# Retention's norm in the first two layers: mean and gate in one VectorE pass, the inverse deviation applied by ScalarE

## The reference

```python
def retention_branch(q, k, v, gate, ret_decay, positions):
    q = rotary(q.reshape(B, S, RET_HEADS, RET_QK_DIM), positions, RET_THETA, RET_QK_DIM)
    k = rotary(k.reshape(B, S, RET_HEADS, RET_QK_DIM), positions, RET_THETA, RET_QK_DIM)
    ...
    o = fwd + bwd                                  # (1, 4 heads, 256 tokens, 512)
    mu = jnp.mean(o, axis=-1, keepdims=True)
    var = jnp.mean(jnp.square(o - mu), axis=-1, keepdims=True)
    o = (o - mu) * lax.rsqrt(var + EPS)
    o = jnp.transpose(o, (0, 2, 1, 3)).reshape(B, S, RET_HEADS * RET_V_DIM).astype(gate.dtype)
    return o * jax.nn.silu(gate)
```

## Time and profile before

| | us |
|---|---|
| median of 3 runs | 3060.93 |
| lowest and highest run | 3060.62, 3064.89 |
| the profiled execution | 3062.25 |
| its span in the trace | 3060.4 |

### The profile page before, as it was taken

The page is one execution under the profiler, slowest core; times in us unless marked ns, Lnnn a source line. Parts: engine busy times, 40 slices in busy tenths (PEclk is TensorE's granted clock), DMA queues, the critical chain, the costliest instruction groups (busy, mean ns, idle before and its releaser), DMA issues. The chain is left out here.

```text
span 3060.4 us, 49236 instructions
## 1 busy us (share of the span) xinstructions
PE 2916.6 (95%) x19366; PEld 2670.4 (87%) x19366; DVE 2271.7 (74%) x4037; ACT 1471.7 (48%) x2425; POOL 742.4 (24%) x374
## 2 busy tenths in 40 slices
PE   7899998999999898999998999999899999999998
PEld 7798887878898787999998988887799999988887
DVE  5878996687899766796568677777599557756665
ACT  3454333445433344545655455554454665445554
POOL 0100000010000000697776000001189776400000
PEclk9999998999999999999999999999899999999999
DMA  6445554543555452454443777873245443455554
GB/s 219 151 152 187 206 207 152 196 167 130 188 204 207 152 203 93 164 183 158 140 136 132 267 255 261 287 285 128 102 163 186 145 138 128 169 180 193 194 195 161
DMA packets 125976, 547.96 MB, mean 179 GB/s; under 512 B 13715, under 2 KB 17972, under 8 KB 101300
## 3 DMA queue, kind: packets, MB, share of 16 engines
q1 hardware_dynamic: 124572, 542.73, 50.8%
q10 hardware_dynamic: 1176, 2.10, 0.4%
HBM read 538.48 MB, written 6.29 MB: 178 GB/s over the span
## 5 line engine op out<-in xcount | busy, mean ns | idle before, releaser
L2011 POOL TENSOR_TENSOR q_lo<-q_raw,q_hi 128x1024 fp32r<-128x1024 f32 x250 | 678.6, 2725 | 226.3 <-ACT q_hi L2120 226.1
L2030 PE MATMUL k_psN<-k_hhi,q_hi 128*128 128x256 f32 x2304 | 665.6, 289 | 19.0 <-POOL q_lo L2011 18.1
L2030 PE MATMUL k_psN<-k_hhi,q_lo 128*128 128x256 f32 x2304 | 651.5, 283 | 0.0
L2030 PE MATMUL k_psN<-k_hlo,q_hi 128*128 128x256 f32 x2304 | 651.4, 283 | 0.0
L2120 ACT ACTIVATE q_hi<-q_raw 128x1024 fp32r<-128x1024 f32 x538 | 566.4, 1053 | 6.8 <-DMA q_raw<-up 4.1
L2030 PEld LDWEIGHTS k_psN<-k_hhi,q_hi 128*128 128x128 f32 x2304 | 441.1, 191 | 25.9 <-POOL q_lo L2011 21.9
L2323 DVE TENSOR_TENSOR q_lo<-q_raw,q_hi 128x1024 fp32r<-128x1024 f32 x288 | 352.8, 1225 | 132.0 <-ACT q_hi L2120 131.4
L2030 PEld LDWEIGHTS k_psN<-k_hlo,q_hi 128*128 128x128 f32 x2304 | 441.6, 192 | 0.0
L2030 PEld LDWEIGHTS k_psN<-k_hhi,q_lo 128*128 128x128 f32 x2304 | 441.1, 191 | 0.0
L744 DVE TENSOR_TENSOR k_wlo<-k_raw,k_whi 128x2048 fp32r<-128x2048 f32 x158 | 360.6, 2286 | 101.6 <-ACT k_whi L569 100.7
L569 ACT ACTIVATE k_whi<-k_raw 128x2048 fp32r<-128x2048 f32 x158 | 301.5, 1913 | 233.2 <-PE f_psA L421 102.9
(11 more groups left out here) (355 smaller groups left out, 5479.2 us busy)
## 6 DMA issues: line engine op xcount, KB each, us to landing
k_raw<-ws SPq DMA_DIRECT2D x180, 1024.0 KB, 4.8
q_raw<-down SPq DMA_DIRECT2D x288, 512.0 KB, 3.4
q_raw<-up SPq DMA_DIRECT2D x256, 512.0 KB, 4.2
k_x<-ada SPq DMA_DIRECT2D x48, 512.0 KB, 3.6
e_ada<-ada SPq DMA_DIRECT2D x48, 512.0 KB, 5.1
out<-k_x SPq DMA_DIRECT2D x3, 1024.0 KB, 3.9
k_x<-out SPq DMA_DIRECT2D x3, 1024.0 KB, 7.0
k_x<-x SPq DMA_DIRECT2D x2, 1024.0 KB, 6.0
```

The source lines that it names most:

```text
L2011: nc.gpsimd.tensor_tensor(lo[:, i % RING, :], raw[:, i % RING, :], hi[:, i % RING, :].bitcast(F32), ALU.subtract).then_inc(S["lo_pool"], 1)
L2030: last = nc.tensor.matmul(psD(n), w, h, start=kt == 0 and i == 0, stop=kt == KT - 1 and i == 2)
```

## The change

VectorE no longer waits for the inverse deviation. It writes (o - mean) x gate in one scalar_tensor_tensor for each half, straight behind the statistics (and the decay arguments, where there are any). ScalarE then multiplies `rog` in place by the inverse deviation, a value for each token, as the scale of a Copy. The count `r_og`, for which `ret_out` waits, is now raised by ScalarE, and VectorE's pass raises `acc_read`.

```diff
                         decay(1)
-                    elif name == "ret_values" and j < 2:
-                        decay(j + 2)
+                    elif name == "ret_values":
+                        if j < 2:
+                            decay(j + 2)
+                        act.wait_ge(S["r_rstd"], j + 1)
+                        for t in range(NT):
+                            act.wait_ge(S["acc_read"], n + t + 1)
+                            nc.scalar.activation(rog[:, t, :], rog[:, t, :], ACT.Copy, scale=RRS[:, 2 * j + t:2 * j + t + 1]).then_inc(S["r_og"], 1)
...
                         if j < 2:
                             decay_arg(j + 2)
-                        dve.wait_ge(S["r_rstd"], j + 1)
+                        own.wait()
+                        dve.wait_ge(S["r_var"], j + 1)
                         for t in range(NT):
-                            V.tensor_scalar(rog[:, t, :], o[t], MV[:, 4 * j + 2 * t:4 * j + 2 * t + 1], RRS[:, 2 * j + t:2 * j + t + 1],
-                                            ALU.subtract, ALU.mult).then_inc(S["acc_read"], 1)
-                        dve.wait_ge(S["acc_read"], n + 2)
-                        for t in range(NT):
-                            V.tensor_tensor(rog[:, t, :], rog[:, t, :], rg[:, j % 2, t, :], ALU.mult).then_inc(S["r_og"], 1)
+                            V.scalar_tensor_tensor(rog[:, t, :], o[t], MV[:, 4 * j + 2 * t:4 * j + 2 * t + 1], rg[:, j % 2, t, :],
+                                                   ALU.subtract, ALU.mult).then_inc(S["acc_read"], 1)
```

## The result

The changed kernel takes **3073.01 us** (median of 8 runs, 3068.76 to 3088.99) where the kernel before took 3062.79 in the runs beside it (median of 8): ratio 1.0033, 95% interval 1.0020 to 1.0046. A second set, 10 runs, gave 3072.27 and 1.0024 (1.0015 to 1.0034) against 33 runs of before. So the change costs 7 to 10 us. The forecast was 3064.1 with a range up to 3069: the sign was right, the size was not, and the time lies outside the range.

A forecast was written before the change was run, and what follows sets the result against it. VectorE, late from the first head on, was taken to set TensorE's restart at `conv_mean`. Lags of 2 x 0.59 + 2 x 0.20 = 1.58 us a layer, 3.2 in two, on 3060.93 gave 3064.1 us, range 3060 to 3069.

The forecast's parts named there:

- the sum: Both first layers: 2 x 1.58 = 3.2 us slower, bounds 2.2 to 4.6, giving 3064.1 us.
- What bounds the kernel: First layers: VectorE runs late from the first head on, and its last tap sets TensorE's restart at `conv_mean`, without slack.
- VectorE's new pass: Each head's norm: one pass per half of 0.75 us, the two ending 1.46 us after the statistics or decay arguments.
- ScalarE in front of L569: Each head: new ScalarE passes delay L569, so L744 is later by 0.59 us (heads 0, 1) and 0.20 (heads 2, 3).
- TensorE's wait before `cgate`: Before `cgate` in the first layer: TensorE's wait for L856 grows from 0.6 to near 2 us, costing nothing in itself.
- POOL: Inverse deviation in heads 2 and 3: POOL's pair still takes 0.19 and 0.69 us beside VectorE's new pass.
- TensorE's clock: Two stalls in each first layer: where the low clock falls is worth up to 0.85 us each, +/-3.4 us, no sign.
- The base: The whole kernel before the change: median of the runs 3060.93 us, to which the forecast effect was added.
- The saving gets through: Rival, chance 0.04: VectorE's 8.9 us a layer removes TensorE's stalls, 7.7 a layer, 15.4 in all, 3045.5 us.
- A longer low clock: Rival, chance 0.12: longer `cgate` wait may bring a low stretch, both restarts may fall badly; 6.6 us slower, 3067.5.
- Nothing moves: Rival, chance 0.03: ScalarE's passes overlap better than counted, or a later wait swallows the lag; 3061 us.
- POOL held up: Rival, chance 0.09: the new passes hold POOL off in each head, 6.6 us a layer, 13.2 slower in all, 3074.1.

The follow-up runs named there:

- half-width passes: The changed kernel with ScalarE's two new passes per head over the left 256 of 512 columns only; 3066.37 us in a single run.
- the taps moved as well: Changed kernel with ScalarE converting the next weights first and convolution taps thinned behind the fourth head, none in the last two units; 3055.27 us (share 0.5), 3054.07 us (0.75).

## Why the prediction was wrong

Three steps failed. The 19 runs of the changed kernel have a median of 3072.3, the forecast was 3064.1. Of the 8.2 us between them, 3.4 are the base, 0.8 are the price of ScalarE's pass, and 2.25 are low clock in the second block, a term that the sum put at nothing. The other 1.8 us are not explained.

**What bounds the kernel: right.** VectorE's last tap before `conv_mean` sets TensorE's restart; the lag added up over the four heads without loss (0.63 + 0.53 + 0.40 + 0.41 = 1.97).

**VectorE's new pass: right.** A pair of 1.40 to 1.41 us where 1.42 was forecast.

**ScalarE in front of L569: right in kind, short in size.** Taken from the end of L990 in head 0 (300.29), L749 starts at +3.93; the forecast said +3.95, and heads 0 and 1 were to lose 0.59 each and lost 0.57. From the end of L1013 in head 2 (378.61), POOL is ready at +1.06 and the first new pass starts at +1.09, as forecast, but L569 starts at +2.34 instead of +2.15 and L749 at +4.27 instead of +4.07. **The term that was mis-sized** is the new pass's price on ScalarE, taken from the Exp: "lasts 0.63 and lets the next start after 0.53". A pass takes 0.72 us, the pair 1.34, not 1.16, and L569 starts 1.25 behind its start, not 1.06. Heads 2 and 3 lose 0.40 each, twice the 0.20 of the sum. The new pass reads a value for each token beside its tile, the Exp does not, and the trace of the kernel before shows ScalarE operations of one size with and without such a value, L665 and L636:

```profile
L665 ACT ACTIVATE f_tmp<-f_tmp,f_stat 128x256 f32<-128x256 f32 x32 | 15.9, 500 | 3.1 <-DVE f_stat L959 3.1
...
L636 ACT ACTIVATE f_rt<-f_rt 128x256 f32<-128x256 f32 x1 | 0.4, 419 | 6.5 <-DVE f_rt L927 6.5
```

The two differ in more than this value, so it is only an estimate: 0.08 us more for each pass would have given 0.61 in place of 0.53; the spacing measured is 0.63 and 0.61. In heads 0 and 1 the error was hidden: the first pass could start at +0.75 in place of +0.83. The stage's lag, 1.97 for 1.58, stayed within the bounds given (1.1 to 2.3), because one of the bounds was just this. The half-width passes showed that it is this term.

**TensorE's wait before `cgate`: too high.** Forecast near 2 us, measured 1.0; the rest of the lag had reached TensorE before, in waits that were not there: 0.5 us at 354 us and 0.3 at 377.

**POOL: right.** Its pair still takes 0.19 and 0.70 us beside the new VectorE pass, which reads PSUM and one SBUF operand. By the Trainium skill, SBUF — State Buffer, section Who interferes with whom, a VectorE instruction with at most one SBUF input does not contend with GpSimd; the trace agrees.

**TensorE's clock: this step failed, and made the range too narrow.** It counted the clock's effect at the four stalls of the first layers only, and put it at nothing for the rest of the kernel, without a reason. In the first block it was small (the block grew by 3.4 to 4.3 us in three traces, of which 3.9 are the lag). The 2.25 us came some 250 to 450 us behind the last changed instruction, in the second block, in all three traces of the changed kernel. Nothing in the trace of before shows that this will come, but it showed stalls with a low clock there, and that a shift can change what follows them should have been a term, as it was for the first layers.

**The base: this step failed too.** The forecast stood on three runs with a median of 3060.93; over 108 runs it is 3064.3. That alone is 3.4 us, more than the forecast effect. With it, the sum reads 3064.3 + 3.9 + 2.25 = 3070.5, against a median of 3072.3 in the 19 runs of the changed kernel. Against the runs of before beside it the effect is 7 to 10 us, two to three times the 3.2 of the sum; so the base alone does not explain the miss.

**The rivals.** *The saving gets through* was ruled out for the change as it stands, rightly. Its size, 7.7 us a layer, held two things that don't come together by themselves: VectorE's 8.9 us of head start is given back at the next head's statistics unless it has other work to do there (-1.5 us a layer measured). With the taps moved as well, the two layers are 8.2 and 8.5 us shorter behind their 1900th and 5000th matmul, and 2.0 come back at low clock between them. *A longer low clock* was the rival nearest to what came, with the wrong place. *Nothing moves* and *POOL held up* did not happen.

## What to carry to other kernels

When an operation moves to an engine that is not busy, ask what that engine issues next and who waits for it: here the relieved engine lost at every head more than it won, because two ScalarE passes of 1.25 us together stood ahead of a conversion, and turning their order changed the sign. A saving on an engine that runs in turns with others is worth only what it can spend before it meets the next of them; look for work to put there before counting it. For effects of a few tenths of a per cent, take the base from many runs, and put a term for what the clock does in parts that aren't touched into the range.

## What the runs showed of the hardware

ScalarE's Copy scaled by a value for each partition, 128x512 from SBUF to SBUF, took 1.34 us in a pair, and the operation behind the pair started 1.25 after its start; at 128x256 the pair took 0.97. The Exp of the shape 128x512, without such a value, took 0.63, and the operation behind it started after 0.53.

The same stall of 2.95 us at 1421 us was followed by full clock in 4 of 4 traces and by 3.4 us of low clock in 13 of 13, beginning between 0.5 us before and 1.1 us behind TensorE's restart. These differ from the four only in the first block, some 250 us earlier and more; the sign and the size of its shift made no difference (first blocks from 14.7 us shorter to 4.3 longer, and one only 0.04 longer), nor did the time from the span's start. What in the shift decides it stays open.

At 2390 us 7 of the 17 traces have a stall of 4.8 us instead of 2.95. In the changed kernel's first trace, VectorE and POOL there:

```profile
2397.05 2.83 DVE L2303 TENSOR_TENSOR e_hot<-e_iota,e_i2T 128x512 f32<-128x512 f32 x1
2400.57 0.68 DVE L2303 TENSOR_TENSOR e_hot<-e_iota,e_i2T 128x512 f32<-128x512 f32 x1
...
2396.95 2.38 POOL L2014 TENSOR_TENSOR q_lo<-q_raw,q_hi 128x1024 fp32r<-128x1024 f32 x1 [0.15 <-ACT q_hi L2123]
```

and in the kernel before:

```profile
2391.71 0.68 DVE L2300 TENSOR_TENSOR e_hot<-e_iota,e_i2T 128x512 f32<-128x512 f32 x1
...
2392.13 2.47 POOL L2011 TENSOR_TENSOR q_lo<-q_raw,q_hi 128x1024 fp32r<-128x1024 f32 x1 [0.68 <-ACT q_hi L2120]
```

The same VectorE operation takes 0.68 us alone (at 2400.57) or where it began 0.42 us before POOL's (at 2391.71), and 2.83 where POOL's began 0.10 us before it: it ends 0.55 us behind POOL's end. In the third trace of the changed kernel it takes 0.68 us at this place, and the stall is 2.95 in the second and the third, so this belongs to the scatter, not to the change. The Trainium skill, SBUF — State Buffer, section Who interferes with whom, says that a VectorE instruction with two SBUF inputs contends with a GpSimd instruction that reads SBUF; the rows agree.
